# A trunk of two layers on one core: the second half of each moving line starts 288 floats behind the first instead of 264

## The reference: what is computed

```
for layer in range(2):
    h = h + 0.5 * swiglu(rmsnorm(h, norm_ff1), w_gate, w_up, w_down)      # 1024 -> 2816 -> 1024
    hn = rmsnorm(h, norm_mix)
    layer 0:  mix = conv_ssm_mixer(hn, even_w_in, ...)                    # in-projection 1024 -> 2048
    layer 1:  mix = window_attention(hn, attn_w_qkv, ...); h, mix without the 16 positions
    h = h + mix
    h = h + 0.5 * swiglu(rmsnorm(h, norm_ff2), ...)
swiglu(x) = (silu(x @ w_gate) * (x @ w_up)) @ w_down
```

## Time and profile before

| | |
|---|---|
| median of two runs | 1880.9 us |
| the profiled execution | 1878.81 us, of which the trace's span is 1877.0 us |
| busy: TensorE matmul, weight load | 1866.7 us (99%), 1766.3 us (94%) |
| busy: VectorE, ScalarE, GpSimd | 957.5 us (51%), 599.9 us (32%), 349.3 us (19%) |
| granted TensorE clock, mean | 1.000 |
| DMA, mean | 100 GB/s |

### The profile page before, as it was taken

The page is one execution under the profiler, slowest core; times in us unless marked ns, Lnnn a source line. Parts: engine busy times, 40 slices in busy tenths (PEclk is TensorE's granted clock), DMA queues, the critical chain, the costliest instruction groups (busy, mean ns, idle before and its releaser), DMA issues.

```text
span 1877.0 us, 33920 instructions
## 1 busy us (share of the span) xinstructions
PE 1866.7 (99%) x13919; PEld 1766.3 (94%) x13919; DVE 957.5 (51%) x1078; ACT 599.9 (32%) x707; POOL 349.3 (19%) x629
## 2 busy tenths in 40 slices
PE   9999999999999999999999999999999999999999
PEld 8999999999999999999999999999988788888887
DVE  5444356568765443344564443445557654434443
ACT  5222222332243222222342222223456442222232
POOL 2888889415230000000000000000012000000000
PEclk9999999999999999999999999999999999999999
DMA  6322444547423322432243223322321233333322
GB/s 183 91 84 84 148 142 128 163 138 187 124 69 90 91 87 85 119 90 73 70 126 90 84 84 101 90 81 73 115 68 46 65 93 94 90 96 102 111 70 87
DMA packets 330785, 188.29 MB, mean 100 GB/s; under 512 B 8152, under 2 KB 323832, under 8 KB 330712
## 3 DMA queue, kind: packets, MB, share of 16 engines
q1 hardware_dynamic: 323024, 166.68, 30.0%
q0 software_dynamic: 7088, 20.38, 3.9%
q10 hardware_dynamic: 600, 0.20, 0.0%
HBM read 174.91 MB, written 11.14 MB: 99 GB/s over the span
## 4 chain that ended last, share of the span: by engine, by line
PE 96%; DVE 2%; issue 1%; ACT 1%; POOL 0%; ACTq 0%; POOLq 0%; DVEq 0%
PE ps L800 79%; PE ps L1041 5%; PE ps L1083 2%; PE ps L1152 2%; PE ps L1102 1%; PE ps L1291 1%; PE ps L1253 1%; PE ps L1193 0%; PE ps L1002 0%; PE ps L1001 0%; PE ps L992 0%; DVE r L1620 0%; PE ps L1214 0%; PE ps L1204 0%; ACT xh L1314 0%
## 5 line engine op out<-in xcount | busy, mean ns | idle before, releaser
L800 PE MATMUL ps<-xh,wh 128*128 128x264 f32 (+1 forms) x2432 | 557.7, 299 | 1.4 <-DVE t_a L1652 1.3
L800 PE MATMUL ps<-xh,wl 128*128 128x264 f32 (+1 forms) x2432 | 556.6, 298 | 0.0
L800 PE MATMUL ps<-xl,wh 128*128 128x264 f32 (+1 forms) x2432 | 556.5, 298 | 0.0
L1591 DVE TENSOR_TENSOR wl<-raw,wh 128x2048 fp32r<-128x2048 f32 x171 | 398.1, 2328 | 170.7 <-ACT wh L1302 170.7
L1302 ACT ACTIVATE wh<-raw 128x2048 fp32r<-128x2048 f32 x172 | 327.5, 1904 | 247.5 <-PE ps L800 205.7
L800 PEld LDWEIGHTS ps<-xh,wh 128*128 128x128 f32 x2432 | 384.9, 188 | 16.4 <-issue 2.7
L800 PEld LDWEIGHTS ps<-xh,wl 128*128 128x128 f32 x2432 | 384.8, 188 | 13.9
L800 PEld LDWEIGHTS ps<-xl,wh 128*128 128x128 f32 x2432 | 384.8, 188 | 13.8 <-issue 0.2
L800 PE MATMUL ps<-act_h,wh 128*128 128x264 f32 (+1 forms) x1232 | 282.2, 298 | 0.0
L800 PE MATMUL ps<-act_h,wl 128*128 128x264 f32 (+1 forms) x1232 | 281.7, 298 | 0.0
L800 PE MATMUL ps<-act_l,wh 128*128 128x264 f32 (+1 forms) x1232 | 281.5, 298 | 0.0
(11 more groups left out here) (313 smaller groups left out, 1683.6 us busy)
## 6 DMA issues: line engine op xcount, KB each, us to landing
raw<-in_ff_w_gate SPq DMA_DIRECT2D x88, 512.0 KB, 3.7
raw<-in_ff_w_up SPq DMA_DIRECT2D x87, 512.0 KB, 4.8
raw<-in_ff_w_down SPq DMA_DIRECT2D x64, 384.0 KB, 3.9
raw<-in_ff_w_down SPq DMA_DIRECT2D x64, 320.0 KB, 3.5
raw<-in_even_w_in SPq DMA_DIRECT2D x16, 512.0 KB, 4.9
raw<-in_attn_w_qkv SPq DMA_DIRECT2D x12, 512.0 KB, 4.4
raw<-in_even_w_out SPq DMA_DIRECT2D x8, 512.0 KB, 4.6
raw<-in_attn_w_o SPq DMA_DIRECT2D x8, 512.0 KB, 4.2
```

The lines of the kernel that those rows point to most:

```text
L800: last = nc.tensor.matmul(ps[:, 2 * pair + hf, 0:nh], w[:, slot, b * P:(b + 1) * P], x[:, k0 + k, c0 + hf * nh:c0 + (hf + 1) * nh], start= ...
L1591: v.tensor_tensor(wl[:, c % 2, :], raw[:, c % 2, :], wh[:, c % 2, :].bitcast(F32), ALU.subtract).then_inc(wl_ready, 1)
```

## The change

The second half of a line of `xh`, `xl`, `act_h` and `act_l` is put 288 floats behind the first, half of the pitch of 576, in place of 264. The 24 floats between the halves stay unused, and so do 24 behind the second half. This holds for the three feed-forwards over 528 positions and for the in-projection of layer 0. The GLU, the out-projection of layer 0, the attention and the last feed-forward keep the whole line. ScalarE and VectorE now write these lines, and read the sources, as 2 by 264 (`spread`, `halves`) in place of 528 in a row. Nothing is added to or taken from any engine's queue: each has as many instructions as before, in the same order, and all buffers keep their addresses.

```diff
-        xh = sb("xh", [P, KD, ROW], F32R)[:, :, 0:L]
+        xh = sb("xh", [P, KD, ROW], F32R)
...
+        def spread(x, k, col):
+
+            return x[:, k, :].rearrange("p (b n) -> p b n", b=2)[:, :, 0:col[1]] if col == ALL else x[:, k, span(operand(col))]
+
+        def half_at(col, hf):
+
+            return hf * (ROW // 2) if col == ALL else col[0]
...
-                                                    x[:, k0 + k, c0 + hf * nh:c0 + (hf + 1) * nh],
+                                                    x[:, k0 + k, half_at(col, hf):half_at(col, hf) + nh],
...
-                            last = nc.tensor.matmul(ps[:, 2 * (p % 2) + hf, 0:L // 2], w[:, slot, b * P:(b + 1) * P], x[:, k, hf * L // 2:(hf + 1) * L // 2],
+                            last = nc.tensor.matmul(ps[:, 2 * (p % 2) + hf, 0:L // 2], w[:, slot, b * P:(b + 1) * P], x[:, k, half_at(ALL, hf):half_at(ALL, hf) + L // 2],
...
-                cols = span(col)
-                nc.scalar.activation(xh[:, d, span(operand(col))], h[:, d, cols], ACT.Copy,
+                into = xh[:, d, span(col)] if m == 4 else spread(xh, d, col)
+                nc.scalar.activation(into, h[:, d, span(col)] if m == 4 else halves(h[:, d, :], col), ACT.Copy,
...
-                            nc.scalar.activation(act_h[:, s + 2 * i, span(operand(col))], t_c[:, cols], ACT.Copy).then_inc(act_h_done[n], 1)
+                            nc.scalar.activation(spread(act_h, s + 2 * i, col), halves(t_c, col), ACT.Copy).then_inc(act_h_done[n], 1)
...
-                            v.tensor_tensor(act_l[:, s + 2 * i, span(operand(col))], t_c[:, cols], act_h[:, s + 2 * i, span(operand(col))].bitcast(F32), ALU.subtract).then_inc(act_ready[n], 1)
+                            v.tensor_tensor(spread(act_l, s + 2 * i, col), halves(t_c, col), spread(act_h, s + 2 * i, col).bitcast(F32), ALU.subtract).then_inc(act_ready[n], 1)
```

More of the change, by code:

```diff
@@ L98, in trunk_program @@
         h = sb("h", [P, KD, L])
-        xh = sb("xh", [P, KD, ROW], F32R)[:, :, 0:L]
-        xl = sb("xl", [P, KD, ROW], F32R)[:, :, 0:L]
-        act_h = sb("act_h", [P, PART[0], ROW], F32R)[:, :, 0:L]
-        act_l = sb("act_l", [P, PART[0], ROW], F32R)[:, :, 0:L]
+        xh = sb("xh", [P, KD, ROW], F32R)
+        xl = sb("xl", [P, KD, ROW], F32R)
+        act_h = sb("act_h", [P, PART[0], ROW], F32R)
+        act_l = sb("act_l", [P, PART[0], ROW], F32R)
         raw = sb("raw", [P, 2, UNITW])
@@ L856, in first_job @@
                         for hf in range(nb):
-                            last = nc.tensor.matmul(ps[:, hf, 0:nh], w[:, 0, k * P:(k + 1) * P], x[:, k, c0 + hf * nh:c0 + (hf + 1) * nh],
+                            last = nc.tensor.matmul(ps[:, hf, 0:nh], w[:, 0, k * P:(k + 1) * P], x[:, k, half_at(col, hf):half_at(col, hf) + nh],
                                                     start=(k == 0 and q == 0), stop=(k == KD - 1 and q == 2))
@@ L871, in second_job @@
                         for hf in range(nb):
-                            last = nc.tensor.matmul(ps[:, 2 + hf, 0:nh], w[:, 0, (KD + k) * P:(KD + k + 1) * P], x[:, k, c0 + hf * nh:c0 + (hf + 1) * nh],
+                            last = nc.tensor.matmul(ps[:, 2 + hf, 0:nh], w[:, 0, (KD + k) * P:(KD + k + 1) * P], x[:, k, half_at(col, hf):half_at(col, hf) + nh],
                                                     start=(k == 0 and q == 0), stop=(k == KD - 1 and q == 2))
@@ L1424, in y_high @@
                 act.wait_ge(yf, YN[f"y{i}"])
-                nc.scalar.activation(act_h[:, 2 * KC + i, :].rearrange("p (c b t) -> p b t c", b=2, t=4),
+                nc.scalar.activation(act_h[:, 2 * KC + i, 0:L].rearrange("p (c b t) -> p b t c", b=2, t=4),
                                      ps[:, 6:8, 0:4 * NCH].rearrange("p b (t c) -> p b t c", t=4), ACT.Copy).then_inc(yth_done, 1)
@@ L1429, in conv_high @@
                 act.wait_ge(dve_mix, 5 * i + 5)
-                nc.scalar.activation(act_h[:, i, :], t_a[:], ACT.Copy).then_inc(yah_done, 1)
+                nc.scalar.activation(act_h[:, i, 0:L], t_a[:], ACT.Copy).then_inc(yah_done, 1)
             split_mix(1)
@@ L1458, in _ @@
                 act.wait_ge(yb_prod, k + 1)
-                nc.scalar.activation(act_h[:, KC + k, :], t_a[:], ACT.Copy).then_inc(ybh_done, 1)
+                nc.scalar.activation(act_h[:, KC + k, 0:L], t_a[:], ACT.Copy).then_inc(ybh_done, 1)
             def project(u0, j0, col, m):
@@ L1611, in scaled_low @@
                 gain = vec[:, GAIN[m] + d:GAIN[m] + d + 1] if isinstance(d, int) else vec[:, bass.ds(d + GAIN[m], 1)]
-                v.scalar_tensor_tensor(xl[:, d, span(operand(col))], h[:, d, cols], gain, xh[:, d, span(operand(col))].bitcast(F32), ALU.mult, ALU.subtract).then_inc(x_ready, 1)
+                whole = lambda x: x[:, d, cols] if m == 4 else spread(x, d, col)
+                v.scalar_tensor_tensor(whole(xl), h[:, d, cols] if m == 4 else halves(h[:, d, :], col), gain, whole(xh).bitcast(F32), ALU.mult, ALU.subtract).then_inc(x_ready, 1)
             def rms(m, col):
@@ L1811, in conv_low @@
                 dve.wait_ge(yah_done, i + 1)
-                v.tensor_tensor(act_l[:, i, :], t_a[:], act_h[:, i, :].bitcast(F32), ALU.subtract).then_inc(ya_ready, 1)
+                v.tensor_tensor(act_l[:, i, 0:L], t_a[:], act_h[:, i, 0:L].bitcast(F32), ALU.subtract).then_inc(ya_ready, 1)
             def input_tables(i):
@@ L1887, in _ @@
                 wait(dve, yb_prod, k)
-                v.tensor_tensor(t_c[:], act_h[:, 2 * KC + k, :].bitcast(F32), act_l[:, 2 * KC + k, :].bitcast(F32), ALU.add).then_inc(dve_mix, 1)
+                v.tensor_tensor(t_c[:], act_h[:, 2 * KC + k, 0:L].bitcast(F32), act_l[:, 2 * KC + k, 0:L].bitcast(F32), ALU.add).then_inc(dve_mix, 1)
                 dve.wait_ge(dve_mix, 5 * KC + k + 1)
@@ L1892, in _ @@
                 dve.wait_ge(ybh_done, k + 1)
-                v.tensor_tensor(act_l[:, KC + k, :], t_a[:], act_h[:, KC + k, :].bitcast(F32), ALU.subtract).then_inc(yb_ready, 1)
+                v.tensor_tensor(act_l[:, KC + k, 0:L], t_a[:], act_h[:, KC + k, 0:L].bitcast(F32), ALU.subtract).then_inc(yb_ready, 1)
             def project(u0, j0, col, m):
```

4 lines of the change are left out of this document (2 added, 2 removed).

## The result

The changed kernel takes 1895.9 us (1895.4 and 1896.4) against 1880.9 us, a ratio of 1.0083 (the medians alone give 1.0080) with a 95% interval of 1.0066 to 1.0100, so 12 to 19 us slower. The forecast had 1867.5 us; the measured time lies above its own range (1861 to 1877) and above the wide one (1846 to 1884), and is within 2% of before. The profiled execution has a span of 1893.6 us, 16.6 more than before.

What follows compares the result with a forecast made beforehand. TensorE, busy 99% of the span, was taken as the bound, through the distance between matmul starts. 5136 pairs × 2.6 ns = 13.4 us saved, writers at 0, gave 1880.9 − 13.4 = 1867.5 us; own range 1861 to 1877, wide range 1846 to 1884.

Steps and rivals of the forecast that it cites:

- the 5136 pairs: Pairs of 264-column matmuls the change reaches: 4704 for gate, up and down, 384 in the in-projection, 48 in the first tiles.
- The writers: ScalarE's and VectorE's lines written as 2 by 264: 0 to +40 ns on ScalarE, covered by waits, put at 0.
- The nearest row: Second half's start in each pair: takes 2.6 ns from a moving start 64 bytes off as the gain, 13.4 us in all.
- the queries' row: Rows 7: matmuls of 512 columns with moving lines 64 bytes off take 229.0 ns, 2.6 ns more than aligned ones.
- The lower bound of my own text: Gain of the second half's new start: nothing, if the 20 ns over a pair are a fixed cost of each matmul.
- the 10 ns over the columns: A matmul of 264 columns takes 120.0 ns where columns alone need 110.0; this excess is all the change can reach.
- Slower: Rival: a start's cost grows with its distance from a multiple of 256 bytes, 20.0 us more, 1900.9 us; chance 0.13.
- No change: Rival: the 20 ns over a pair are fixed, or 256 bytes is the boundary that matters; 1880.9 us; chance 0.24.
- The full excess: Rival: the second half pays up to 6.5 ns now and nothing after; 1847.5 us; chance 0.15.
- Rows 8: Ten matmuls with moving operand aligned and stationary blocks 64 bytes off take 233.0 ns, 6.6 ns more.
- The rule I weighed: SBUF lines of 16 bytes, an access pays at a new line: the shift does nothing, sum 1880.9 us.

Runs made afterwards that it cites:

- e8: The changed kernel, complete, with the second half 312 floats behind the first in place of 288: 1881.0 us against 1881.0, ratio 1.0004.
- e1: Kernel of before, line 800's second half read from another start in each of twelve stages, products wrong: 240.0 to 246.6 ns a pair.
- e2: Kernel of before, both halves' starts moved by stage at line 800, in two stages the weights' too, products wrong: 240.0 to 246.6 ns a pair.
- e5: Kernel of before, weights read from other starts by stage at line 800, some second halves from 256, products wrong: 240.0 to 246.7 ns a pair.
- e6: Kernel of before, both halves' starts moved by stage with weights aligned, products wrong: 240.0 to 246.7 ns a pair; 512 columns 228.9 to 233.3 ns.
- e7: Kernel of before, other numbers of moving and weight columns by stage, products incomplete: halves from 0 and 256 take 246.6 to 240.0 ns a pair.
- e3: Kernel of before, lines written whole, second half read from float 224 in all 5136 pairs, products wrong: 1897.2 us against 1880.6, ratio 1.0089.
- e10: Kernel of before, lines written whole, second half read from float 256 in all 5136 pairs, products wrong: 1912.2 us against 1880.3, ratio 1.0169.
- e11: Kernel of before, complete, with 32 unused floats in front of the weights, so their blocks start 128 bytes off: 1918.8 us against 1880.3, ratio 1.0195.

## Why the prediction was wrong

**What held.** TensorE is the bound and only the distance between starts counts; the 5136 pairs, 5136 × 3.33 = 17.1 us against a span longer by 16.6. The writers and the gap cost nothing that can be measured (e8 and the rows of the changed kernel). What keeps its layout kept its pace.

**The step that failed** is "The nearest row: 2.6 ns for a moving start that is 64 bytes off. I take this ... It takes the cost of a start to end at a multiple of 128". It priced the old start of the second half by the queries' row and thereby supposed that it had a price. It had none that a start could take away: 240.0 ns a pair is the least that any of the settings with 264 moving and 128 weight columns showed (e1, e2, e5, e6), and it stays with fewer weight columns (e7). The lower bound of my own text was the truth about before: of the 10 ns over the columns no start tried took any away. What was missing was a price for the new start: the pair's three starts, of first half, second half and weights, decide together, and 0, 32 and 0 behind cost 3.3 ns a pair. Two readings of the prediction were slips as well, without weight in its sum: it says that no matmul reads a moving line at 32 bytes, and every second half before did; and TensorE's longest wait was 1.5 us (line 929), not 1.4.

Open: something beyond the three starts enters. Two of the sets have two paces (16 behind for the second half, 240.0 and 243.3; weights 32 behind, 244.4 and 246.7), and inside a stage the pace changes at an idle moment of TensorE. What the pause resets no run shows. The sets on which the verdict rests kept one pace in all feed-forward stages over a whole kernel, pauses included: 240.0 before and in e8, 243.3 after and in e3, 246.6 in e10.

**The rivals.** *Slower* had 0.13 and 1900.9 us, near the 1895.9 measured, but for a wrong reason: a price by distance would make 256 the cheapest and 312 dear, and they are the dearest (e10) and as cheap as before (e8). *No change* had the right account of the old start and missed the new one's. *The full excess* supposed that an aligned 264 would cost the share of 512, 116.7 ns; e10 has 123.3. Rows 8 held a hint that I read past. There the moving operand was aligned and the weights were not, 512 columns leave twice the time that a weight load needs, and yet 6.6 ns were lost. A price for the weights' start in matmuls which the weight load cannot bound suggests that the weights' start and the moving one are not priced apart, and then aligning the moving start alone has no reason to help.

**The Trainium skill.** The rule I weighed, in "SBUF — State Buffer", section "Door 1: The DMA port swizzle" (lines of 16 bytes), gave no change; starts at multiples of 16 bytes differ here by up to 6.7 ns a pair, so it is not the rule for this price. "TensorE: Matmul & The Clock Gate" says in its section "Step-by-step: what each phase is for" that matmul and weight load have read ports of their own and that a load takes no read bandwidth from the running matmul. For these float32r matmuls the load beside them is not free: its start moves a pair by up to 6.7 ns (e5, e11), and with halves from 0 and 256 the pair loses 6.6 ns at 128 weight columns and none at 32 (e7). The measurement decides, though no run shows at which port or part of SBUF the time goes.

## What to carry to other kernels

An aligned start need not be the cheap start: in these float32r matmuls, each with a weight load beside it, the starts of moving operand and weights are priced together, and the price has to be measured for the combination, best by giving each stage of one kernel another start, and then for the whole kernel, since in two of the sets the pace changed at a pause. Before padding for alignment, find the floor: here the pair already stood at the least that any start gave, so there was nothing to win. A small row in which only one operand's start differs is worth more than a rule, but it prices its own combination and not the next one.

## What the runs showed of the hardware that I had not expected

- Float32r matmuls with 128 weight columns cost 120.0 ns at 256 columns and at 264, 114.2 at 248 and 125.3 at 272 (there with all starts at 0): some steps are free and some are not.
- 512 columns cost 226.7 ns with moving operand and weights at 0 behind; at 4, 8, 12 and 16 behind for the moving one 231.7, 233.3, 232.0 (last stage) and 228.9. So 512 columns are cheapest aligned, of what was tried, and 264 columns dearest.
- The same instructions with the same starts ran at 246.7 and at 244.4 ns a pair in one stage of e11, with an idle moment of 0.7 us between.
